# Taking GpSimd out of the second half of a two-layer trunk kernel: VectorE does its passes, TensorE turns the last head's sums, and the rotary angles go to GpSimd

## The reference

```python
ang = rope_pos[..., None] * inv_freq;  cos, sin = jnp.cos(ang), jnp.sin(ang)
# layer 0
c_q, c_kv, k_rope, z = split(h @ w_in)                 # 384, 256, 32, 1024 columns
q = rms_norm(c_q, q_g) @ w_uq                          # its last 32 of 96 per head are rotated
c_kv = rms_norm(c_kv, kv_g);  k_nope = c_kv @ w_uk;  v = c_kv @ w_uv
o = softmax(where(mask, (q_nope @ k_nope.T + q_rope @ k_rope.T) * scale, -1e30)) @ v
h = layer_norm(ALPHA * h + (o * silu(z)) @ w_o, ln_g[0], ln_b[0])
# layer 1
b_gate, c_gate, u, z = split(h @ w_in, 4)              # 4 x 1024 columns
cu = pad(c_gate * u);  conv = sum(cu[k:k+L] * conv_w[k] for k in range(3))
h = layer_norm(ALPHA * h + (b_gate * conv * silu(z)) @ w_out, ln_g[1], ln_b[1])
return h[16:]
```

## Time and profile before

| | us |
|---|---|
| median of 3 runs | 2696.84 (2693.94, 2696.84, 2700.38) |
| the profiled execution | 2696.37 |
| its span in the trace | 2694.6 |
| TensorE busy | 2575.2 (96% of the span) |
| VectorE busy | 1953.5 (72%) |
| ScalarE busy | 1449.8 (54%) |
| GpSimd busy | 754.6 (28%), in 343 instructions |
| TensorE's mean granted clock | 0.983 of full speed |

### The profile page before, as it was taken

How to read it: one execution, slowest core, us unless ns; L and a number is a source line. 1 busy time by engine, 2 the same in 40 slices (tenths; PEclk the granted TensorE clock), 3 DMA queues, 4 the chain that set the end, 5 groups by cost and what they waited for, 6 DMA issues and landing times. The chain is left out here.

```text
span 2694.6 us, 48122 instructions
## 1 busy us (share of the span) xinstructions
PE 2575.2 (96%) x17332; PEld 2421.1 (90%) x17332; DVE 1953.5 (72%) x3793; ACT 1449.8 (54%) x3539; POOL 754.6 (28%) x343
## 2 busy tenths in 40 slices
PE   6999999999999999999999979997999999999898
PEld 5899999999999989999999968877999999999786
DVE  6556761139898889899989858896887756665565
ACT  4334322248888888888888851133445445444211
POOL 0000000013344545443334305474551200000254
PEclk8999999999999999999999989998999999999999
DMA  4545454312243333333333335735454444553343
GB/s 151 190 144 191 148 162 120 111 45 46 52 102 81 86 79 92 89 80 72 72 82 73 65 105 163 252 104 207 156 172 163 166 154 146 177 192 127 130 140 117
DMA packets 247200, 337.07 MB, mean 125 GB/s; under 512 B 88448, under 2 KB 184576, under 8 KB 234432
## 3 DMA queue, kind: packets, MB, share of 16 engines
q1 hardware_dynamic: 229296, 325.67, 40.5%
q10 hardware_dynamic: 17680, 8.46, 1.1%
HBM read 224.54 MB, written 108.98 MB: 124 GB/s over the span
## 5 line engine op out<-in xcount | busy, mean ns | idle before, releaser
L1206 DVE TENSOR_TENSOR b_pt_lo<-b_transposed,b_pt_hi 128x384 fp32r<-128x384 f32 (+4 forms) x784 | 429.1, 564 | 50.7 <-ACT b_pt_hi L1107 47.1
L1107 ACT ACTIVATE b_pt_hi<-b_transposed 128x384 fp32r<-128x384 f32 (+4 forms) x784 | 382.5, 502 | 124.1 <-PE b_transposed L1137 111.5
L1097 ACT ACTIVATE ground<-b_ring,ground 128x384 f32<-128x384 f32 (+7 forms) x784 | 436.2, 561 | 19.6 <-DVE ground L1196 11.3
L1191 DVE TENSOR_REDUCE ground<-b_ring 128x1 f32<-128x384 f32 (+7 forms) x784 | 409.5, 528 | 33.4 <-PE b_ring L45 13.8
L1137 PE MATMUL b_transposed<-identity,ground 128*128 128x128 f32 (+2 forms) x2448 | 379.9, 272 | 14.0 <-DVE b_pt_lo L1206 8.7
L1137 PEld LDWEIGHTS b_transposed<-identity,ground 128*128 128x128 f32 (+2 forms) x2448 | 279.8, 134 | 62.1 <-issue 28.5
L1154 PE MATMUL b_o_ps<-b_pt_hi,b_v 128*128 128x256 f32 (+2 forms) x1280 | 334.2, 292 | 0.7 <-DVE b_pt_lo L1206 0.7
L1155 PE MATMUL b_o_ps<-b_pt_lo,b_v 128*128 128x256 f32 (+2 forms) x1280 | 312.7, 281 | 0.0
L43 PE MATMUL b_ring<-region 128*128 128x384 f32 (+7 forms) x784 | 301.4, 385 | 3.9 <-DVE b_transposed L1167 2.4
L43 PE MATMUL p_banks<-p_x_hi,big 128*128 128x258 f32 x896 | 254.7, 284 | 9.2 <-DVE big L568 8.3
L45 PE MATMUL b_ring<-region 128*128 128x384 f32 (+7 forms) x784 | 259.0, 330 | 0.0
(11 more groups left out here) (222 smaller groups left out, 6763.1 us busy)
## 6 DMA issues: line engine op xcount, KB each, us to landing
ground<-x_a SPq DMA_DIRECT2D x23, 1032.0 KB, 5.6
ground<-w_conv SPq DMA_DIRECT2D x32, 512.0 KB, 3.9
c_tiles<-w_conv SPq DMA_DIRECT2D x32, 512.0 KB, 3.7
c_ln<-weight_sums SPq DMA_DIRECT2D x16, 1024.0 KB, 7.5
c_tiles<-weight_sums SPq DMA_DIRECT2D x16, 1024.0 KB, 7.0
weight_sums<-c_tiles SPq DMA_DIRECT2D x9, 1024.0 KB, 7.9
keys<-ground SPq DMA_DIRECT2D x64, 129.0 KB, 5.1
queries<-ground SPq DMA_DIRECT2D x64, 129.0 KB, 2.9
```

Source lines behind the costliest of these rows:

```text
L1097: nc.scalar.activation(p[0:rows, n % PSLOTS, 0:w], banks[0:rows, n % RING, 0:w], ACT.Exp, bias=nmax[0:rows, tile % 8:tile % 8 + 1], accum_ ...
L1107: nc.scalar.activation(turned(pt_hi, g, u, nb)[:, :, tile_columns(u, j)], tb[:, n % 2, 0:nb, 0:rows], ACT.Copy).then_inc(pt_hi_done, 1)
L1191: ins = nc.vector.tensor_reduce(top, bank[0:rows, 0:w], AX, ALU.max, negate=(chunks == 1))
L1206: nc.vector.tensor_tensor(lo, tb[:, n % 2, 0:nb, 0:rows], hi.bitcast(F32), ALU.subtract).then_inc(pt_split, 1)
```

## The change

**Stage P.** Eight of the eleven angle passes go to GpSimd; VectorE keeps the three range reductions, now behind the first chunk's key (`split_weights`) and ahead of the mean. The first `latent(0)` stands ahead of `split_x(2)` on VectorE, and on ScalarE ahead of the sines, with the split of chunk 2 and the copies behind them. Two weight pieces move from step ("p",1) to ("o",0). **Stage B.** TensorE transposes the last head's inverse sums, ScalarE copies them, and SP stores them as rows. **Stage C.** SP loads the gated heads and the gate first and waits for the last head's output and sums only before those loads; ScalarE's queue starts the sums' loads of tiles 0 and 1. The affine vectors are applied by two VectorE instructions that also normalise (`normalise_rows`). Statistics of a half are taken right behind its residual. `turn` comes one tile later instead of two. **Stage D.** `sum_weights` and `sum_window` are VectorE's, at places written into its order. GpSimd has no instruction in C, D and E. **Stage E.** SP's wait for the last results moves from the end of stage C/D to behind stage E's first loads. The last tile is normalised and stored in two halves.

```diff
@@ stage P
-PIECES_AT = {("p", 0): [("uk", 0), ("uk", 1)], ("p", 1): [("uv", 0), ("uv", 1)],
+PIECES_AT = {("p", 0): [("uk", 0), ("uk", 1)], ("o", 0): [("uv", 0), ("uv", 1)],
...
+            pool.wait_ge(const_in, 64)
+            then(nc.gpsimd.tensor_scalar(ang, ppos, float(META), rc[:, 0:1], ALU.add, ALU.mult))
+            then(nc.gpsimd.tensor_scalar(turns, ang, 1 / TURN, rc[:, 1:2], ALU.mult, ALU.add))
+            then(nc.gpsimd.tensor_scalar(turns, turns, ROUND, -ROUND, ALU.add, ALU.add))
+            pool.wait_ge(reduced, 1)
+            then(nc.gpsimd.tensor_scalar(ang, ang, rc[:, 2:3], None, ALU.add))
+            then(nc.gpsimd.tensor_scalar(turns, ang, 1 / TURN, ROUND, ALU.mult, ALU.add))
+            then(nc.gpsimd.tensor_scalar(turns, turns, -ROUND, -TURN, ALU.add, ALU.mult))
+            then(nc.gpsimd.tensor_tensor(ang, ang, turns, ALU.add))
+            nc.gpsimd.tensor_scalar(ang, ang, PI_BELOW, -PI_BELOW, ALU.min, ALU.max).then_inc(angle, 1)
...
                     if g == 1:
                         root(0)
-                        split_x(2)
                         latent(0)
-                        copies(1)
-                        split_weights(PIECES_AT["p", 1])
                         act.wait_ge(angle, 1)
...
+                        split_x(2)
+                        copies(1)
@@ stage B
+                sp.wait_ge(r_copied, 1)
+                sp.dma_start(r_d[HEADS - 1:HEADS, META:T].rearrange("a (j p) -> (a j) p", p=P), r_t[0:NT, :]).then_inc(r_out, 16)
+                sp.dma_start(r_d[HEADS - 1:HEADS, 0:META], r_t[NT:NT + 1, 0:META]).then_inc(r_out, 16)
...
                 elif letter == "T":
+                    if n == LAST_SUMS_AT:
+
+                        pe.wait_ge(r_done, HEADS)
+                        nc.tensor.transpose(banks[0:NT + 1, 0, 0:P], r_sb[:, (HEADS - 1) % 2, :], ident[:, :]).then_inc(r_turned, 1)
@@ stages C to E
+def normalise_rows(nc, then, y, stats, gb, affined):
+
+    then(nc.vector.scalar_tensor_tensor(y, y, stats[:, 12:13], gb[0], ALU.subtract, ALU.mult))
+    nc.vector.scalar_tensor_tensor(y, y, stats[:, 16:17], gb[1], ALU.mult, ALU.add).then_inc(affined, 1)
...
-LAG_C = 2
+LAG_C = 1
...
+SUM_PART_AT = {1: 5, 5: 6, 6: 7, 7: 3}
...
-WINDOW_AT, SUMS_AT = WINDOW_TILE + 3, WINDOW_TILE + 5
+WINDOW_AT, SUMS_AT = WINDOW_TILE + 3, WINDOW_TILE + 4
...
-TURN_15, TURN_16 = (0, 6), (1, 7)
+TURN_16 = (1, 6)
...
-            sp.wait_ge(g_out, 16 * (NPAIRS // 2))
             sp.wait_ge(taps_in, 16)
...
+            act.wait_ge(r_out, 32 * HEADS)
+            load_sums(act, 0)
+            load_sums(act, 1)
...
-                    if k == 2:
+                    if k == KD - 2:
                         turn(i - LAG_C)
...
+                nc.vector.tensor_tensor(to, a, b, ALU.subtract).then_inc(h_summed, 1)
...
+                nc.vector.tensor_tensor(to, a, b, op).then_inc(w_summed[n % 2], 1)
...
+                if SECOND_AT.get(i + 1) in W_SUM:
+                    sum_weights(1, SECOND_AT[i + 1])
+                if n and n + 1 < PER_PASS and m in SUM_PART_AT:
+                    sum_weights(n + 1, SUM_PART_AT[m])
+                p, at = n // PER_PASS, n % PER_PASS
+                if m == 2 and 5 <= at < 9 and p + 1 < PASSES:
+                    sum_window(p + 1, at - 5)
...
+            sp.wait_ge(g_out, 16 * (NPAIRS // 2))
             with sp.Fori(1, NTE // 2) as i:
```

More of the change, by code:

```diff
@@ L1215, with half_stats @@
 NTC = TP // P
+def half_stats(nc, y, stats, half):
+    nc.vector.bn_stats(stats[:, 6 * half:6 * half + 6], y[:, half * HALF:half * HALF + HALF])
 def row_variance(nc, dve, then, y, stats, var_done):
-    for half in range(2):
-        nc.vector.bn_stats(stats[:, 6 * half:6 * half + 6], y[:, half * HALF:half * HALF + HALF])
     dve.drain()
```

229 lines of the change are left out of this document (101 added, 128 removed).

## The result

The changed kernel ran in 2656.66 us (median of 4 runs, 2651.44 to 2658.76), the kernel before in 2695.39 beside it. The ratio is 0.9846, with a 95% interval of 0.9827 to 0.9865: 1.5% faster. The span of its profiled execution is 2657.0 us, 37.6 less than the 2694.6 of before.

The account below looks back on a forecast made before the run. TensorE was taken to bound the kernel, leaving only its standing and lower-clock time to win. Terms +1.0 - 5.5 - 23.9 - 7.6 - 2.1 - 1.6 = -39.7 us took 2696.37 to 2656.7, range 2640 to 2680.

Parts of the forecast that it names:

- What bounds it: Whole kernel: TensorE is busy nearly throughout, so only its standing or lower-clock time can be won; GpSimd delays VectorE in D.
- Stage P, +1.0: Head of the kernel: GpSimd's angle passes and the new order cost 1.0 us net, range -2.4 to +4.
- B to C, -5.5: Edge between stages B and C: storing the last head's sums as rows saves 5.5 us, range -6.5 to -4.5.
- D's first pass, -23.9: 1791 to 1963 us: GpSimd's lengthening of VectorE disappears, saving 23.9 of 38.6 us, range -38.6 to -12.
- the waits that I kept: 1791 to 1963 us: waits of order remain for product (1,1), `c11(1)` and the first pair's convolution, 8.2 us of standing.
- Next part of D, -7.6: 1963 to 2150 us: the 5.7 us wait and most other standing go, saving 7.6 us, range -10.5 to +10.
- (A): D's first pass: VectorE becomes the bound, 15.2 us a block instead of 13.4, +25 us, 2682; chance 0.13.
- Rest of D, 0: 2150 to 2498 us: no change, since no sums are read off GpSimd there.
- D to E and tail, -2.1 and -1.6: Stage E's edge saves 2.1 us by moving SP's wait; its tail saves 1.6 through the last tile's shorter work.
- (D): Stage D: each sum holds VectorE's queue 1.585 us, 16.7 us a block, +46 us, slower at 2703; chance 0.05.
- (B): D's first pass: loads, stores and ScalarE's order set the gaps, so all four long waits stay, +11.6, 2668; chance 0.12.
- (C): D's first pass: the gaps vanish and nothing is kept, 14.7 us less, 2642; chance 0.08.

## Why the prediction was right, point by point

**What bounds it.** That only TensorE's standing and its lower clock could be won, and that VectorE was late through GpSimd's instructions, held: every part found is a gap of TensorE or the clock behind one, and the run with idle subtractions shows that the lock is enough to cause such gaps. The prediction had argued it from one pair of rows and the 2.2 us of L1788.

**Stage P, +1.0.** The term held, +0.4 in the mean over nine traces against two, though the first pair of traces said +3.6. The bracket for the latent's restart (37.8 to 41 us) holds eight of nine traces; they have 37.7 to 39.1. The five passes behind the last reduction take 9.1 us together, where I had 9.5, but not as I had it: three take 1.05 to 1.24 us, not the 1.9 of L52, and L357 and the two-input L360 take 2.92 and 2.40. The 2.3 us of an earlier latent are right: 36.2 and 35.9 with the passes on VectorE against 38.3 in the run with stage P as before. But 38.3 is also 1.2 us later than the 37.08 of the same code in the trace that I started from, and no run shows the 33.9 of a stage without the lock. What failed is the second restart. It came not between 52.3 and 54.7 us but at 48.9, and not for what the sines and keys give but for the squares of chunk 1 (L591), and a third wait of 2.38 us for the moved weight pieces (`region` L584) was not in the sum. So the size of this term is partly luck. The Trainium skill's estimate of 0.9 us for a pass ("GPSIMD Engine Reference", section "Elementwise — side-by-side cycle accounting") was nearer to the three short passes than L52, but the term that followed from it, -2.4, was wrong.

**B to C, -5.5.** -5.9 us. That the store is what is waited for, and that the end of the stage is late next, both hold.

**D's first pass, -23.9.** -24.5 us, with C. Of the waits that I kept, (1,1)'s was 3.3 us (3.2 in the sum), the one for c_tiles 3.4 (2.6), and the one at L1831 of c_gt 3.5 where I had 2.4 for `c11(1)`; two small ones for ScalarE, 2.0 together, were not in the sum. So 12.2 us are kept instead of 8.2. The lower clock made that good. The three stretches are there at 0.50, but 3.4 us long each and not 4.35, which keeps 5.1 us instead of 6.5 (columns as in the first rows of this part, the clock third from the end):

```profile
1814.73:1818.13 3.40, 3.40 (x14) 3.40 (x13) 1.72 (x3) 1.40 (x3) 0.00 (x0) 0.50 0.01 2
1842.04:1845.44 3.40, 3.40 (x13) 3.40 (x13) 1.26 (x2) 1.46 (x2) 0.00 (x0) 0.50 0.31 118
1852.28:1855.68 3.40, 3.19 (x11) 3.23 (x12) 3.37 (x7) 1.10 (x3) 0.00 (x0) 0.50 0.04 14
```

And more was to be won than I had: the 0.91 over 172 us in the earlier trace rows is 15.5 us lost, not the 13.05 from the earlier trace rows. So standing gave 13.3 us, not 17.3, and the clock 10, not 6.6. The sum was near because these errors have opposite signs.

**Next part of D, -7.6.** -8.0. VectorE's 11.2 us a block, 12.8 with a window's sum, would be 12.0 in the eight blocks above; it measured 11.1. The slack of 2.2 us a block that rival (A) was weighed with was right in kind: doubling the sums used it up and brought 16.6 us. The last sum of weights starts at 2017 us, so what follows up to 2112 has no sums at all; I had counted it as if it had.

**Rest of D, 0.** +1.9 in the first trace. Most of it is the clock behind a gap of 1.90 us at 2255, 0.76 from 2257 to 2264 us; the kernel before had a gap of 1.57 there and a clock of 1.00. In the second trace of the changed kernel the same gap of 1.90 us is followed by a clock of 1.00, and the part is +0.6. So most of it is spread.

**D to E and tail, -2.1 and -1.6.** -2.4 and -2.0. The wait itself is 2.05 us. No run takes the tail apart.

**The rivals.** (D) needed sums at 1.45 us; they took 0.69. (A) needed 15.2 us a block; a pair took 26.0 to 27.3, some 13.3 a block. (B) was right in part, since 12.2 us of waits of order stay, but as to the gain it is refuted by the sums on GpSimd: with loads, stores and orders as in the changed kernel, 23.8 us come back. (C) asked for nothing to be kept, and 12.2 us were.

**What would be different on average.** The hit, 2656.7 against a median of 2656.66, is luck beyond some two us: beside it the medians differ by 38.7 us, and by 37.3 on the chip of the second measurement (2688.29 and 2650.98), where 39.7 was forecast. Stage B ended between 1583.1 and 1594.4 us in the nine traces with the changed stage P, and the first of them was the latest. The changed kernel alone is 2656.66 on one chip and 2650.98 on another.

## What to carry to other kernels

Before GpSimd is given elementwise work beside a busy VectorE, count what reads SBUF on both. Here VectorE's instruction with two SBUF inputs was mostly held until GpSimd's was over (3.56 us instead of 0.69), and TensorE paid for it where it waited for what is queued behind. Work that only writes cost nothing here. VectorE had slack in the sense of busy time per block, 2.2 us of 13.4, and could take the work over at half the duration (0.69 us instead of 1.59 a sum); the gain is the lock, not the moved work.

## What the runs showed that was not expected

- A GpSimd pass of 128x1032 with one SBUF input, L355, took 4.56 us in all nine traces, with VectorE idle for much of it, where others of its form took 1.05 to 1.3. That GpSimd is held by VectorE as well is not shown by it; L357 (2.92 us) may be a case.
- A VectorE instruction with one SBUF input, L626 (a tensor-scalar of 128x258), took 1.03 us beside GpSimd against 0.30, and ended 0.15 us after the GpSimd pass beside it in all nine traces. So not only those with two SBUF inputs were held.
- L624, with two SBUF inputs, ran wholly beside L357 and took 0.43 us, as alone. Two inputs beside a reading GpSimd don't always mean a wait, and what decides which engine stands is open.
- Stage B takes from 1001.3 to 1009.3 us in fourteen traces, more than the change of stage P is worth. Its code differs among them only in the last head's sums, and the two longest are the trace of before and the first one of the changed kernel. A difference of a few us in an early stage cannot be read from one pair of traces.
- A gap of 1.90 us of TensorE was followed by a clock of 0.76 over 7 us in one trace and of 1.00 in another of the same kernel. One of 1.88 us was followed by 0.69 over 5.5 us in the run with GpSimd's reads, and one of 1.89 by 1.00 before the change.
